# Gate and up projections of a decoder layer with the weights as the stationary operand

## The reference

```
x = x + rmsnorm(mix, post_mix_norm[layer])
h = rmsnorm(x, pre_ffn_norm[layer])
f = (jax.nn.silu(h @ w_gate[layer]) * (h @ w_up[layer])) @ w_down[layer]
x = x + rmsnorm(f, post_ffn_norm[layer])
```

## Time and profile before

| | us |
|---|---|
| time, median of 3 runs (318.72 to 318.75) | 318.73 |
| span of the profiled execution, first to last instruction | 316.7 |
| TensorE busy | 307.7 (97%) |
| VectorE busy | 180.9 (57%) |
| ScalarE busy | 150.9 (48%) |
| POOL busy | 24.6 (8%) |
| mean granted clock of TensorE, share of 2.4 GHz | 0.997 |

### The profile page before, as it was taken

How to read it: one execution, slowest core, us unless ns; L and a number is a source line. 1 busy time by engine, 2 the same in 40 slices (tenths; PEclk the granted TensorE clock), 3 DMA queues, 4 the chain that set the end, 5 groups by cost and what they waited for, 6 DMA issues and landing times.

```text
span 316.7 us, 4110 instructions
## 1 busy us (share of the span) xinstructions
PE 307.7 (97%) x1432; PEld 247.1 (78%) x1432; DVE 180.9 (57%) x255; ACT 150.9 (48%) x248; POOL 24.6 (8%) x27
## 2 busy tenths in 40 slices
PE   6999999999999999999999999999999999999992
PEld 3788867778888888778888888888888888888881
DVE  2858447675467497899555555544444454551426
ACT  5887654436409164676444444444433333340322
POOL 2020045000002000540000000000000000000001
PEclk9999999999999999999999999999999999999998
DMA  7999994405451553279955555555655655400003
GB/s 212 405 406 378 411 395 138 148 26 184 150 155 46 199 155 112 71 220 314 340 179 174 179 193 185 167 178 191 199 199 199 199 197 192 141 0 0 0 2 132
DMA packets 17518, 58.35 MB, mean 184 GB/s; under 512 B 1998, under 2 KB 2518, under 8 KB 17505
## 3 DMA queue, kind: packets, MB, share of 16 engines
q1 hardware_dynamic: 17136, 57.06, 52.3%
q0 software_dynamic: 368, 1.11, 1.0%
HBM read 57.10 MB, written 1.06 MB: 184 GB/s over the span
## 4 chain that ended last, share of the span: by engine, by line
PE 90%; DVE 4%; POOL 2%; DMA 2%; ACT 1%; issue 0%; SPq 0%; DVEq 0%
PE bank L942 26%; PE bank L944 26%; PE bank L943 25%; PE bank L952 4%; DMA raw<-in_w_in 2%; PE bank L969 1%; POOL xs L442 1%; PE bank L1043 1%; PE bank L1041 1%; PE bank L973 1%; PE bank L977 1%; DVE d_lo L867 1%; DVE res L933 1%; DVE w_lo L860 1%; PE bank L1075 1%; DVE res L927 1%
## 5 line engine op out<-in xcount | busy, mean ns | idle before, releaser
L942 PE MATMUL bank<-w_hi,a_hi 128*128 128x512 f32 x256 | 101.7, 397 | 0.0
L944 PE MATMUL bank<-w_hi,a_lo 128*128 128x512 f32 x256 | 100.1, 391 | 0.0
L943 PE MATMUL bank<-w_lo,a_hi 128*128 128x512 f32 x256 | 99.7, 390 | 0.0
L944 PEld LDWEIGHTS bank<-w_hi,a_lo 128*128 128x128 f32 x256 | 48.0, 188 | 10.5
L942 PEld LDWEIGHTS bank<-w_hi,a_hi 128*128 128x128 f32 x256 | 48.1, 188 | 10.3 <-issue 0.7
L608 ACT ACTIVATE sil<-bank,rstd 128x256 f32<-128x256 f32 x22 | 10.4, 473 | 95.8 <-PE bank L944 93.4
L943 PEld LDWEIGHTS bank<-w_lo,a_hi 128*128 128x128 f32 x256 | 48.1, 188 | 9.8
L860 DVE TENSOR_TENSOR w_lo<-raw,w_hi 128x1024 fp32r<-128x1024 f32 x40 | 49.5, 1276 | 6.5 <-ACT w_hi L593 6.5
L875 DVE SCALAR_TENSOR_TENSOR hid<-bank,rstd,sil 128x256 f32<-128x256 f32 x22 | 10.6, 484 | 74.3 <-ACT sil L608 74.3
L672 DVE TENSOR_TENSOR w_lo<-raw,w_hi 128x1024 fp32r<-128x1024 f32 x32 | 40.3, 1281 | 17.9 <-ACT w_hi L456 17.9
L593 ACT ACTIVATE w_hi<-raw 128x1024 fp32r<-128x1024 f32 x40 | 40.4, 1057 | 0.0
(11 more groups left out here) (116 smaller groups left out, 299.2 us busy)
## 6 DMA issues: line engine op xcount, KB each, us to landing
raw<-in_w_gu SPq DMA_DIRECT2D x44, 512.0 KB, 4.5
raw<-in_w_dn SPq DMA_DIRECT2D x22, 512.0 KB, 4.7
raw<-in_w_in SPq DMA_DIRECT2D x20, 512.0 KB, 9.1
raw<-in_w_out SPq DMA_DIRECT2D x8, 512.0 KB, 3.2
raw<-in_w_in SPq DMA_DIRECT2D x8, 256.0 KB, 5.5
xs<-in_x SPq DMA_DIRECT2D x2, 512.0 KB, 8.2
bias<-bias_row POOLq DMA_DIRECT2D x1, 1024.0 KB, 9.8
out<-res SPq DMA_DIRECT2D x4, 256.0 KB, 2.0
```

The lines of the kernel that those rows point to most:

```text
L942: pe.matmul(acc, hi, wh, start=first, stop=False)
L943: pe.matmul(acc, hi, wl, start=False, stop=False)
L944: return pe.matmul(acc, lo, wh, start=False, stop=last)
```

## The change

Group 0 is computed as before, except that `hid` of it lacks the factor on the up side. The other 2560 hidden columns become 20 blocks of 128 (b = 2 to 21). In a block the weights are stationary and tokens move: for each of 8 pieces of k a matmul with stationary `w_hi` over 512 moving columns, `a_hi` of all 256 tokens beside `a_lo` of all 256 (`a_both`), and one with stationary `w_lo` over the 256 columns of `a_hi`, into the low half of the same bank. Gate has one bank and up another; blocks alternate between two pairs of banks. The low half of a bank then holds hi x hi + lo x hi, the high half hi x lo, and the two are added outside TensorE: ScalarE copies the high half to SBUF (`cross_copy`), VectorE adds the low half to it. The result has hidden columns on the partitions, as `down` needs it, so there is no transpose. The token's factor is now a value per column: `factor_row` makes a row of factors on all partitions with one fp32 matmul of ones by two diagonals (`diagonal`), VectorE multiplies gate by it, and the factor on the up side moves behind the down projection (`rf`, and the last products). Units of weights are laid out for this on the host; loops are written out.

```diff
+BASE = N_IN + N_OUT + GU
+FFN = [("gu", 2 * b + i) for b in (FIRST,) for i in range(2)] + [("dn", b) for b in range(FIRST)]
+for _b in range(FIRST + 1, NB):
+    FFN += [("gu", 2 * _b), ("gu", 2 * _b + 1), ("dn", _b - 1)]
+FFN += [("dn", NB - 1)]
+N_ALL = BASE + len(FFN)
+LEAD_FFN = 6
...
-        a_hi = sb("a_hi", [P, NK, S], F32R)
-        a_lo = sb("a_lo", [P, NK, S], F32R)
+        a_both = sb("a_both", [P, NK, 2, S], F32R)
+        a_hi, a_lo = a_both[:, :, 0, :], a_both[:, :, 1, :]
...
-            h_hi = sb("h_hi", [P, NT, DN, P], F32R, scope=ffn)
-            h_lo = sb("h_lo", [P, NT, DN, P], F32R, scope=ffn)
-            sil = sb("sil", [P, NT, FG], scope=ffn)
-            hid = sb("hid", [P, NT, FG], scope=ffn)
+            h_hi = sb("h_hi", [P, HBUF, S], F32R, scope=ffn)
+            h_lo = sb("h_lo", [P, HBUF, S], F32R, scope=ffn)
             res = sb("res", [P, NT, D], scope=ffn)
+            cross = sb("cross", [P, 2, 2, S], scope=ffn)
+            sil = sb("sil", [P, 2, S], scope=ffn)
+            hid = sb("hid", [P, 2, S], scope=ffn)
...
+        pb = [bank01, bank45]
+        pr_row = bank67
...
+            pool.memset(ones[:, :], 1.0).then_inc(ones_ready, 1)
...
+            def diagonal(t):
+                wait_factor(act, X1_, t)
+                if t == 0:
+                    act.wait_ge(ident_loaded, 16)
+                act.activation(diag[:, t, :], ident[:, :], ACT.Copy, scale=rstd[:, X1_, t:t + 1]
+                               ).then_inc(diag_ready, 1)
+            def cross_copy(b, up):
+                i = b - FIRST
+                act.wait_ge(w_used, w_place("gu", 2 * b + up) + 1)
+                if i >= 2:
+                    act.wait_ge(sum_ready[up], i - 1)
+                act.activation(cross[:, up, b % 2, :], pb[b % 2][:, up, S:2 * S], ACT.Copy
+                               ).then_inc(cross_ready[up], 1)
+            def silu_block(b):
+                i = b - FIRST
+                act.wait_ge(z_ready, i + 1)
+                if i < 2:
+                    act.wait_ge(hid_ready[i], 1)
+                else:
+                    act.wait_ge(hb_ready, i - 1)
+                act.activation(sil[:, b % 2, :], cross[:, 0, b % 2, :], ACT.Silu).then_inc(s_ready, 1)
+            def h_hi_block(b):
+                act.wait_ge(hb_ready, b - FIRST + 1)
+                if b >= HBUF:
+                    act.wait_ge(d_used, b - HBUF + 1)
+                act.activation(h_hi[:, b % HBUF, :], hid[:, b % 2, :], ACT.Copy).then_inc(hbhi_ready, 1)
...
+            hi_ffn(0)
             a_hi_part(1, 0)
-            hi_gu(1, 1, 1)
+            hi_ffn(1)
             a_hi_part(1, 1)
             x1_squares(0)
-            hi_gu(1, 2, 1)
-            wait_factor(act, X1_, 0)
-            silu(0, 0)
-            hi_gu(1, 3, 1)
+            hi_ffn(2)
+            diagonal(0)
+            silu_rows(0)
+            hi_ffn(3)
             x1_squares(1)
-            hi_dn(0, 0, 0)
-            wait_factor(act, X1_, 1)
-            silu(0, 1)
-            h_hi_part(0, 0)
-            hi_dn(0, 1, 0)
-            group(1, 1)
-            with act.Fori(2, NF - 2, 2) as g:
-                group(g, 2)
-                group(g + 1, 3)
-            group(NF - 1, NF - 1, more=False)
-            h_hi_part(NF - 1, 1)
+            hi_ffn(4)
+            diagonal(1)
+            silu_rows(1)
+            h_hi_rows(0)
+            hi_ffn(5)
+            h_hi_rows(1)
+            for b in range(FIRST, NB):
+                nxt = LEAD_FFN + 3 * (b - FIRST)
+                cross_copy(b, 0)
+                for i in range(nxt, min(nxt + 1, len(FFN))):
+                    hi_ffn(i)
+                silu_block(b)
+                for i in range(nxt + 1, min(nxt + 2, len(FFN))):
+                    hi_ffn(i)
+                cross_copy(b, 1)
+                h_hi_block(b)
+                for i in range(nxt + 2, min(nxt + 3, len(FFN))):
+                    hi_ffn(i)
+            act.wait_ge(rf_ready, 1)
             for t in range(NT):
                 for c in range(2):
                     act.wait_ge(f_done, 2 * t + c + 1)
-                    squares(F_, t, c, pf[t][:, c, :])
+                    squares(F_, t, c, pf[t][:, c, :], scale=rf[:, t:t + 1])
...
+            def z_block(b):
+                i = b - FIRST
+                dve.wait_ge(cross_ready[0], i + 1)
+                dve.tensor_tensor(cross[:, 0, b % 2, :], pb[b % 2][:, 0, 0:S], cross[:, 0, b % 2, :], ALU.add
+                                  ).then_inc(sum_ready[0], 1)
+                dve.wait_ge(sum_ready[0], i + 1)
+                dve.tensor_tensor(cross[:, 0, b % 2, :], cross[:, 0, b % 2, :], r_row[:, :], ALU.mult
+                                  ).then_inc(z_ready, 1)
+            def hidden_block(b):
+                i = b - FIRST
+                dve.wait_ge(cross_ready[1], i + 1)
+                dve.wait_ge(s_ready, i + 1)
+                if i < 2:
+                    dve.wait_ge(h_turned[i], 1)
+                else:
+                    dve.wait_ge(hblo_ready, i - 1)
+                dve.tensor_tensor(cross[:, 1, b % 2, :], pb[b % 2][:, 1, 0:S], cross[:, 1, b % 2, :], ALU.add
+                                  ).then_inc(sum_ready[1], 1)
+                dve.wait_ge(sum_ready[1], i + 1)
+                dve.tensor_tensor(hid[:, b % 2, :], cross[:, 1, b % 2, :], sil[:, b % 2, :], ALU.mult
+                                  ).then_inc(hb_ready, 1)
+            def h_lo_block(b):
+                dve.wait_ge(hbhi_ready, b - FIRST + 1)
+                dve.tensor_tensor(h_lo[:, b % HBUF, :], hid[:, b % 2, :], h_hi[:, b % HBUF, :].bitcast(F32),
+                                  ALU.subtract).then_inc(hblo_ready, 1)
...
             residual(0)
             a_lo_part(1, 0)
-            lo_gu(1, 0, 1)
+            lo_ffn(0)
             a_lo_part(1, 1)
             residual(1)
             factor(X1_, 0, 10)
-            lo_gu(1, 1, 1)
-            hidden(0, 0)
-            lo_gu(1, 2, 1)
-            lo_gu(1, 3, 1)
+            lo_ffn(1)
+            lo_ffn(2)
+            hidden_rows(0)
+            lo_ffn(3)
             factor(X1_, 1, 12)
-            lo_dn(0, 0, 0)
-            hidden(0, 1)
-            h_lo_part(0, 0)
-            lo_dn(0, 1, 0)
-            group(1, 1)
-            with dve.Fori(2, NF - 2, 2) as g:
-                group(g, 2)
-                group(g + 1, 3)
-            group(NF - 1, NF - 1, more=False)
-            h_lo_part(NF - 1, 1)
+            lo_ffn(4)
+            hidden_rows(1)
+            h_lo_rows(0)
+            wait_factor(dve, X1_, NT - 1)
+            dve.tensor_scalar(rf[:, :], rstd[:, X1_, :], 1.0 / math.sqrt(D), None, ALU.mult).then_inc(rf_ready, 1)
+            lo_ffn(5)
+            h_lo_rows(1)
+            dve.wait_ge(row_done, 1)
+            dve.tensor_copy(r_row[:, :], pr_row[:, 0, 0:S]).then_inc(row_ready, 1)
+            dve.wait_ge(row_ready, 1)
+            for b in range(FIRST, NB):
+                nxt = LEAD_FFN + 3 * (b - FIRST)
+                z_block(b)
+                for i in range(nxt, min(nxt + 1, len(FFN))):
+                    lo_ffn(i)
+                hidden_block(b)
+                for i in range(nxt + 1, min(nxt + 2, len(FFN))):
+                    lo_ffn(i)
+                h_lo_block(b)
+                for i in range(nxt + 2, min(nxt + 3, len(FFN))):
+                    lo_ffn(i)
...
-                    dve.tensor_tensor(res[:, t, cols], pf[t][:, c, :], gf[:, cols], ALU.mult
-                                      ).then_inc(res_part, 1)
+                    dve.scalar_tensor_tensor(out=res[:, t, cols], in0=pf[t][:, c, :],
+                                             scalar=rstd[:, X1_, t:t + 1], in1=gf[:, cols],
+                                             op0=ALU.mult, op1=ALU.mult).then_inc(res_part, 1)
...
+            def factor_row():
+                pe.wait_ge(ones_ready, 1)
+                pe.wait_ge(diag_ready, NT)
+                pe.wait_ge(x1_ready, 2)
+                pe.matmul(pr_row[:, 0, 0:S], ones[:, :], diag[:, :, :].rearrange("p t i -> p (t i)"),
+                          start=True, stop=True).then_inc(row_done, 1)
+            def turned_block(b, up):
+                i = b - FIRST
+                n, slot = unit_n("gu", 2 * b + up), w_place("gu", 2 * b + up) % RING
+                if i == 0:
+                    pe.wait_ge(hid_ready[up], 1)
+                elif i == 1:
+                    pe.wait_ge(hlo_ready[up], 1)
+                else:
+                    pe.wait_ge(sum_ready[up], i - 1)
+                pe.wait_ge(lo_ready, n + 1)
+                acc = pb[b % 2][:, up, :]
+                for k in range(NK):
+                    wh, wl = w_hi[:, slot, k * P:(k + 1) * P], w_lo[:, slot, k * P:(k + 1) * P]
+                    if k == NK - 1:
+                        pe.matmul(acc[:, 0:S], wl, a_hi[:, k, :], start=False, stop=False)
+                    ins = pe.matmul(acc, wh, a_both[:, k, :, :].rearrange("p h i -> p (h i)"),
```

(76 more changed lines are left out.)

219 lines of the change are left out of this document (86 added, 133 removed).

## The result

The changed kernel takes 322.62 us (median of 4 runs, 321.87 to 323.83), the kernel before beside it 318.74 (318.72 to 318.75): a ratio of 1.0118, 95% interval 1.0089 to 1.0147, so 3.9 us or 1.2% slower. The forecast was 320.8 with a range of 317.4 to 323.4. The direction and the range held; the size was 1.8 us too small, and the forecast's own likeliest range, 318.6 to 321.9, was missed.

A forecast was written before the change was run, and what follows sets the result against it. TensorE, busy 307.7 of 316.7 us, was taken to bound the kernel. Blocks -3.1, factor row +0.5, start +2.9, end +1.7 and last products +0.1 sum to +2.1 on 318.73: 320.8 us, range 317.4 to 323.4.

The forecast's parts named there:

- Second wait: Start of the feed-forward part: TensorE, with less work in front, waits 3.3 us for group 0's second hidden tile.
- Last wait: End of the feed-forward part: TensorE waits for the hidden values before down of block 21, +1.7 us.
- Factor row: One added plain fp32 matmul of 256 columns on TensorE that makes the row of factors, +0.5 us.
- No wait at any steady block: Steady part: copies, adds and products on ScalarE and VectorE stay covered and cost nothing; uncovered, 2.6 us per block.
- rival A: Blocks: 256-column matmuls step at 0.112 us, the 2 ns surplus goes, POOL goes first; 316.7 us, chance 0.13.
- rival C: Blocks: weight loads of the small matmuls are exposed; about 356 us, 330 if a third shows; chance 0.05.
- rival D: Start and end: the two new waits are about half as long, +1.5 and +1.0; 318.7 us, chance 0.15.
- rival B: Start: TensorE's clock falls in the new 3.3 us wait, costing +1.5 to 2; 322.6 us, chance 0.12.
- The first wait: Start: group 0's first hidden tile is ready later behind VectorE's extra low part, +0.4 us.
- The block: Steady part on TensorE: a block takes 8.31 us against 8.464 for a half group, -3.1 us over 20.
- The surplus: Steady part: 512-column matmuls take 0.229 us, 2 ns more than in the quiet stretch, laid to ScalarE being busy.
- the 0.8 of before: Start, kernel before: TensorE loses 0.8 us because the second hidden tile's factor is late; gone after the change.

The follow-up runs named there:

- VectorE's order: The changed kernel with VectorE's first hidden tile of group 0 ahead of one low part of weights, as in the kernel before: 321.26 us, ratio 1.0079.
- grouped kernel: The changed kernel with the eight 256-column matmuls of each half block issued in a row instead of alternating with the 512-column ones: 322.29 us, ratio 1.0102.
- last tiles reordered: The changed kernel with the first three down tiles of block 20, then of block 21, ahead of the fourth of each: 322.54 us, ratio 1.0120.
- more work at the start: The changed kernel with VectorE's order and block 3's gate half computed ahead of the second tile's transposes: 319.55 us, ratio 1.0030.
- three edits: The changed kernel with grouped matmuls, last tiles reordered and more work at the start together: 317.82 us, ratio 0.9982 to the kernel before.
- Memset: The kernel before with only POOL's 128x128 memset of ones added: 318.69 us, ratio 1.0005.
- loops: The kernel before with only its hardware loops written out: 318.73 us, ratio 1.0004.

## Why the forecast was right, and where it was off

**Direction, and the waits: right.** The forecast said that TensorE's saving would be less than two new waits. Second wait: forecast 3.3, measured 3.1 (step 3.33 less one step). More work in front of it, with VectorE's order, took it away and 3.1 us of time with it. Last wait: forecast 1.7, measured 1.78. Factor row: 0.5, and 0.4. No wait at any steady block, no block of 8.15 (rival A), no exposed load (rival C) and no half-long waits (rival D). That the number lies in the range is in part the range's width: its upper end, 323.4, is there for rival B.

**The first wait: the size nearly, the cause wrong.** Forecast +0.4 through VectorE's second low part ahead of the first tile; measured +0.2. Taking that low part away left the step at 1.40; putting the diagonal behind the SiLU as well brought it to 1.17. The diagonal on ScalarE set it; the forecast had it "behind VectorE's delay". The forecast let the low part wait out POOL's factor; it ran beside it instead and ended 0.7 us behind it (135.60 and 134.88), where the forecast had 1.1. So it came 0.1 ahead of the SiLU, and taking away the diagonal alone would have won little (not run). The low part did lengthen the second wait, by 0.62 us, where the forecast had 1.0.

**The block: the mis-sized term.** Forecast 28 x 0.229 + 16 x 0.119 = 8.31; measured 8.360, of which the 12 down steps take 0.227 (not 0.229) and the pair 0.353 (not 0.348). That is 16 x 0.005 - 12 x 0.002 = +0.05 a block, 1.0 us over 20: -2.1 where -3.1 was forecast. The step that failed is "The surplus falls in the stretch where ScalarE is busy ... I keep 0.229 for every 512-column matmul". ScalarE is busy in after's down steps too, and they are quiet; the surplus comes after a short matmul, and in the new block every second matmul is one. With the small ones in a row the block is 8.307, which is what was priced (8.31): 0.119 to 0.120 for a small one and 0.228 in the mean for a big one. By the gap formula that the Trainium skill gives for a single matmul ("TensorE: Matmul & The Clock Gate", section "Back-to-back issue gap"), cited in the forecast, the steps would be 0.216 and 0.109; here they are 0.227 and 0.120, 11 ns more.

**The clock: a rival with a chance of 0.12 that came true in about a third of the executions, and in one of after's four.** The forecast summed without it. The fall took 1.7 us in the profiles that show 3.4 us of it, and 2.9 in the grouped kernel's, where the clock was low from 140.05 to 146.87 and TensorE back at work from 141.08: half of 5.8. Without the wait no profile shows it before the end of the run. It explains the run of 323.83 (clock 0.991) and part of the median.

**Not forecast: +1.0 before the changed part.** In nine of the thirteen profiles here those transposes start between 26.07 and 26.84; in four (after, last tiles reordered, more work at the start, three edits) between 26.96 and 27.45, and there ScalarE waits 1.1 us or more for a landing. Memset and loops are excluded by their runs. Five kernels with the change are early, so the change doesn't bring it each time; but all four late ones have the change, and none of the four without it is late. The new layout's own loads do not start before that point, so I take it for scatter of the load queue; that is argued, and what sets the landing stays open. Since it scatters, it belongs to the profiled run (323.0) more than to the median.

**Not where the forecast had it: the 0.8 of before.** It read those 0.8 us as a wait for the second hidden tile. The transposes at 140.74 show that they were lost behind it. They are gone in after all the same, so the sum isn't touched.

So, from 320.8: block +1.0, first and second wait -0.4, factor row -0.1, last wait +0.2 and after the last matmul +0.2: 0.9 of the 1.8. The other 0.9 lies between the clock and the landing in the first stretch; the runs don't split these two for the median.

## What to carry to other kernels

Ask of a change that shortens the work on the bounding engine what that work was covering: here the same 20 blocks were 3.9 us slower or 2.1 faster. Of these 6 us 1.1 is the order of widths inside the block; most of the rest is what TensorE was given to do while the first and last hidden tiles were made. A wait costs its length plus, in some executions, a stretch at half the clock, so a scatter of 2 us that one kernel has and the other has not is itself a sign of a wait to look for. And matmuls of unlike widths are better issued in runs of one width than alternating.

## What the runs showed of the hardware that was not expected

- A 512-column matmul right behind a 256-column one steps at 0.236 us where its like steps at 0.227; behind a single short one the following 18 steps are 0.232, behind eight small ones in a row five are. Why is open; work of ScalarE beside them isn't it, for after's down steps are at 0.227 beside it.
- With a wait of 3.1 us the granted clock fell to 0.50 in some executions of one kernel and not in others, and stayed there for 3.4 us in one profile and 6.8 in another. Behind a wait of 2.5 us (VectorE's order alone, a step of 2.71) it fell too, for 3.4 us; one of 0.6 (in front of block 3's gate) did not in 7 executions.
- POOL's factor for one tile, 128x1, takes 1.46 us while VectorE makes a low part beside it and 0.55 where VectorE stands; at the end it takes 0.55 also beside a VectorE product that reads a PSUM bank (313.24 to 313.98 in after). The two residual adds took 4.18 us in after against 3.50 before, next to one more low part on VectorE, and 3.56 with that low part moved behind the first tile.
